# Router and transposes of a tile woven between the dense products of the next output projection unit

## The chip, the cores and the metric

One core of one Trainium2 chip runs the whole layer as one program. The metric is the device time of one execution in microseconds (us); the median of several runs is compared.

## The reference, cut to what matters

The kernel computes one encoder layer for two groups of tokens, 256 (prompt) and 512 (sample), that share all weights. The change lies in the second half of it:

```
def encoder_layer(x, ...):
    h = rms_norm(x, norm1_g)
    proj = h @ w_in                                     # 2048 -> 4896
    mla_out = mla_mixer(...)                            # 8 heads of 128
    gdn_out = gdn_mixer(...)                            # 8 heads of 128
    x = x + concatenate([mla_out, gdn_out]) @ w_o       # 2048 x 2048, the output projection
    x = x + ec_moe(rms_norm(x, norm2_g), w_router, w_gate, w_up, w_down)

def ec_moe(x, w_router, w_gate, w_up, w_down):
    C = 2 * T // 16                                     # 32 prompt, 64 sample tokens an expert
    aff = softmax(xt @ w_router)                        # T x 16
    gates, idx = top_k(aff.T, C)                        # each expert chooses its C tokens
    xe = xt[idx]
    h = silu(xe @ w_gate) * (xe @ w_up)                 # 16 experts, 2048 -> 1024
    ye = (h @ w_down) * gates
    out = zeros_like(xt).at[idx].add(ye)
```

All numbers are float32. The 16 experts' weights are 403 MB, read once.

## The kernel before

The 768 tokens are six tiles of 128. After the two mixers, `output_and_route` multiplies by w_o, adds the residual, normalises, computes the router's logits and lets each expert choose its tokens; `moe` then runs the experts one after another, their weights streamed in units of 2 MB through a ring of six buffers.

The output projection is cut into units (j, t): tile t of tokens by slice j of 512 columns of w_o, 16 matmuls with 128 rows of contraction each. Two records stand in the trace for one such matmul. The list `UNITS` has 24 of them, numbered u = 0 to 23: slice 0 of five tiles (four of which have only their last two contractions left), slices 1 to 3 of the same five tiles, and last the four slices of the sixth tile (ORDER[-1], tile 1), in the order 2, 3, 0, 1. `FIRST` is 15, the number of the first unit of slice 3: unit 15 + o finishes tile o of the order. Two buffers hold slices of w_o; slices 0 and 1 are therefore loaded a second time for units 22 and 23.

Each engine has its own program, written out by hand as a loop over the units; counting semaphores order them. Around a finished tile o this is the chain:

- TensorE: `accumulate(u)` (L1992), into PSUM bank u % 3.
- VectorE: `add(u)` (L2082) adds the residual. ScalarE: `square(u)` (L2193) sums squares, `rms(o)` (L2199, L2201) makes the scale.
- VectorE: `norm(o)` (L2094) writes the normed tile to `xn`, two buffers, both for the router and for the rows that go out.
- TensorE: `transposes(o)` (L2003), 16 transposes of 128 x 128 into PSUM banks 3 to 6, four to a bank; `store(o)` copies them to `xnT`, banks 3 and 5 on VectorE (L2103), 4 and 6 on ScalarE (L2208).
- TensorE: `router(o)` (L2014), 16 matmuls with 16 columns each, two records each, into bank 7. VectorE and ScalarE make the softmax (L2108 to L2120, L2214), `affinity(o)` (L2021) transposes it back.
- After five tiles, VectorE runs `top` (L2132 to L2135) for the sample tokens, eight rounds of maximum, index and replace. It stands ahead of the additions of units 22 and 23.
- The sixth tile is routed slice by slice by `last_transposes` (L2028) and `last_router` (L2042), then `top` runs for the prompt tokens.

The loop of TensorE before the change is, for each u: `accumulate(u)`; with o = u - 16 then `affinity(o - 2)`, `router(o - 1)`, `transposes(o)`, `last_transposes(o - 5)`, each where its index is in range. VectorE's order for each u is add, gain, softmax(o - 1), store(o), norm(o + 1), store_affinity(o - 2), top; ScalarE's is square, exponent(o - 1), store(o), rms(o + 1), store_last.

SyncE's program issues the DMAs in order: the residual, the slices of w_o, then for each tile `rows_out(o)` (L1945, L1946; waits for the norm of tile o, sends the normed and the plain rows, 1 MB each), and after `rows_out` of the fifth tile the second loads of slices 0 and 1, `load_w` (L1939), which wait until 21 and 22 units are done. Behind them come the first three units of expert 0, when unit 22 and unit 23 are done (L1972). The next units are requested by the following block, at L2338.

Of the kernel before, what the change touches and what calls it, by code (L numbers as in the profile page):

```python
# [20 lines left out]
P = 128  # L21
# [3 lines left out]
NT = T // P  # L25
TILES_P = SP_ // P
KD = D // P
# [3 lines left out]
H = 8  # L31
# [60 lines left out]
class Kernel:  # L92
# [18 lines left out]
    def sb(self, name, shape, dt=F32, ctx=None):  # L111
        return (ctx or self.ctx).enter_context(self.nc.sbuf_tensor(name, shape, dt))

    def sem(self, name, ctx=None):
        return (ctx or self.ctx).enter_context(self.nc.semaphore(name))
# [1738 lines left out]
def output_and_route(k):  # L1854

    nc, a, ps = k.nc, k.a, k.psum
# [20 lines left out]
    FIRST = (GR - 1) * (NT - 1)  # L1877
    done_at = lambda o: FIRST + o if o < NT - 1 else NU - 1
    with ExitStack() as c:
# [4 lines left out]
        xn = sb("xn", [P, 2, D])  # L1884
# [25 lines left out]
        s_acc = sem("output_projected")  # L1910
# [7 lines left out]
        s_tp = sem("xn_transposed")  # L1918
        s_td = sem("xnT_stored_vector")
        s_ta = sem("xnT_stored_scalar")  # L1920
        s_lg = sem("logits")
# [13 lines left out]
        with nc.Block() as block:  # L1935
# [43 lines left out]
            @block.tensor  # L1979
            def _(pe):  # L1980
                def accumulate(u):
                    j, t = UNITS[u]
                    if u == 0:
                        pe.wait_ge(k.s_mix, 32)
                    if u % (NT - 1) == 0 or u > GR * (NT - 1):
                        loads = 1 if j < 2 else 2
                        pe.wait_ge(s_w[j % 2], 16 * (loads if u <= GR * (NT - 1) or j >= 2 else 3))
                    if u >= 3:
                        pe.wait_ge(s_x2, u - 2)
                    q0 = PART_HEADS if j == 0 and t in PARTS else 0  # L1990
                    for q in range(q0, 2 * H):
                        last = nc.tensor.matmul(ps[:, u % 3, :], mixT[:, q, t * P:(t + 1) * P], wo[:, j % 2, q, :],  # L1992
                                                start=(q == q0), stop=(q == 2 * H - 1))
                    last.then_inc(s_acc, 1)

                def transposes(o):
                    pe.wait_ge(s_xn, o + 1)
                    for b in range(4):
                        if o:
                            pe.wait_ge((s_td, s_ta)[b % 2], 2 * o - 1 + b // 2)  # L2000
                        for j in range(4):
                            m = 4 * b + j
                            last = nc.tensor.transpose(ps[:, 3 + b, j * P:(j + 1) * P], xn[:, o % 2, m * P:(m + 1) * P], k.ident)  # L2003
                        last.then_inc(s_tp, 1)

                def router(o):
                    if o == 0:
                        pe.wait_ge(s_r, 48)
                    else:
                        pe.wait_ge(s_le, o)  # L2010
                    for q in range(KD):
                        if q % 4 == 0:
                            pe.wait_ge((s_td, s_ta)[(q // 4) % 2], 2 * o + 1 + q // 8)
                        last = nc.tensor.matmul(ps[:, 7, 0:NE], xnT[:, q, :], wr[:, q, :], start=(q == 0), stop=(q == KD - 1))  # L2014
                    last.then_inc(s_lg, 1)

                def affinity(o):
                    pe.wait_ge(s_af, o + 1)
                    if o:
                        pe.wait_ge(s_atc, o)  # L2020
                    nc.tensor.transpose(ps[0:NE, 7, P:2 * P], aff[:, ORDER[o], :], k.ident).then_inc(s_at, 1)  # L2021

                def last_transposes(p):
                    j = SLICES[p]
                    pe.wait_ge(s_xg, p + 1)
                    pe.wait_ge((s_td, s_ta)[j % 2], 2 * (NT - 1) - 1 + j // 2)
                    for m in range(4):
                        last = nc.tensor.transpose(ps[:, 3 + j, m * P:(m + 1) * P],  # L2028
                                                   xg[:, 512 * j + m * P:512 * j + (m + 1) * P], k.ident)
                    last.then_inc(s_tp, 1)  # L2030

                def last_router(p):
                    if p == 0:
                        pe.wait_ge(s_le, NT - 1)
                        pe.wait_ge(s_atc, NT - 1)
                    if p < 3:
                        pe.wait_ge(s_ta, 2 * (NT - 1) + p + 1)
                    else:
                        pe.wait_ge(s_td, 2 * (NT - 1) + 1)
                    for m in range(4):  # L2040
                        q = 4 * SLICES[p] + m
                        last = nc.tensor.matmul(ps[:, 7, 0:NE], xgT[:, q, :], wrp[:, q, :], start=(p == 0 and m == 0),  # L2042
                                                stop=(p == 3 and m == 3))
                    if p == 3:
                        last.then_inc(s_lg, 1)

                for u in range(NU):
                    accumulate(u)
                    o = u - FIRST - 1
                    if 2 <= o <= NT:  # L2050
                        affinity(o - 2)
                    if 1 <= o <= NT - 1:
                        router(o - 1)
                    if 0 <= o < NT - 1:
                        transposes(o)
                    if NT - 1 <= o <= NT:
                        last_transposes(o - NT + 1)
                pe.wait_ge(s_sel, 1)
                nc.tensor.transpose(ps[0:CS, 0, 0:NE], idxf[:, 0:CS], k.ident[0:NE, 0:NE]).then_inc(s_selt, 1)
                last_transposes(2)  # L2060
                last_router(0)
                last_router(1)
                last_transposes(3)
                last_router(2)
                last_router(3)
                affinity(NT - 1)
                pe.wait_ge(s_sel, 3)
                nc.tensor.transpose(ps[0:CP, 7, 256 + NE:256 + 2 * NE], idxf[:, CS:CT], k.ident[0:NE, 0:NE]).then_inc(s_selt, 1)
# [513 lines left out]
```

## Time and profile before

| | |
|---|---|
| median of 3 runs | 3069.76 us (3069.10 to 3069.83) |
| the profiled execution | 3071.65 us, span 3069.8 us |
| granted TensorE clock, mean | 0.976 of full speed |
| TensorE busy | 2891.6 us, 94% of the span |
| output projection and routing | 1625.4 to 1966.6 us |
| experts | 1966.6 to 3069.8 us |

The stretch that the change touches begins at 1813.14 (the first transposes) and ends at 1947.18. Times in rows are microseconds from the start of the span. The granted clock is 1.00 at 2.4 GHz and 0.50 at 1.2 GHz; PE is TensorE, PEld its weight loads, DVE VectorE, ACT ScalarE, SPq SyncE's queue of DMAs. In the rows the program's names of buffers stand: xT or xnT for transposed tiles, wbuf for the buffers that hold w_o and the expert weights, square for the identity matrix.

### The profile page before, as it was taken

The numbers are of one execution on the slowest core, as the hardware profiler recorded it, in microseconds if no ns is written. First come the engines' busy times: TensorE is split into PE (matmuls) and PEld (weight loads), VectorE is DVE, ScalarE is ACT, GpSimd is POOL, SyncE is SP. The second block draws the span as 40 slices with busy tenths as digits, with TensorE's granted clock in tenths as the row PEclk, the third lists the DMA queues.
The fourth block names the chain that finished last, engine by engine and source line by source line (L and its number), as shares of the span: only waits on it lengthen the run. The fifth ranks groups of instructions, "written<-read, shape, count | busy, mean of one in ns | idle before, by whom it ended". The sixth has DMA issues, their size and how long they took to land. (4 is left out here: it accounts for less than half of the span.)

```text
span 3069.8 us, 45507 instructions
## 1 busy us (share of the span) xinstructions
PE 2891.6 (94%) x19449; PEld 1451.7 (47%) x19449; DVE 890.9 (29%) x1613; ACT 512.7 (17%) x1333; POOL 409.8 (13%) x400
## 2 busy tenths in 40 slices
PE   8999999999999999998899999799999999999997
PEld 4544455555676666665564456333332232322232
DVE  1000344421764664675761022300000000000000
ACT  4110355412213213214111001100000000000000
POOL 0000111104114214215210000000110000011001
PEclk9999999999999999998999999899999999999998
DMA  5120200030211211103205113799999999999996
GB/s 184 55 73 21 68 28 28 11 118 28 56 53 38 56 42 49 56 15 118 72 22 212 55 55 155 289 404 397 386 390 381 395 395 394 393 394 387 391 396 250
DMA packets 140611, 561.01 MB, mean 183 GB/s; under 512 B 15216, under 2 KB 47816, under 8 KB 87240
## 3 DMA queue, kind: packets, MB, share of 16 engines
q1 hardware_dynamic: 131527, 534.08, 45.1%
q0 software_dynamic: 8960, 25.17, 3.9%
q8 instruction: 92, 1.51, 0.2%
q14 instruction: 32, 0.25, 0.0%
HBM read 524.25 MB, written 34.96 MB: 182 GB/s over the span
## 5 line engine op out<-in xcount | busy, mean ns | idle before, releaser
L2398 PE MATMUL psum<-wbuf,xeT 128*32 128x512 f32 x3120 | 356.8, 610 | 35.2 <-DMA wbuf<-in_w_up 32.3
L1222 PE MATMUL psum<-xT,wbuf 128*128 128x512 f32 x720 | 337.6, 606 | 0.3 <-PEq L612 0.3
L2398 PE MATMUL psum<-xT,xeT 128*32 128x512 f32 x3024 | 330.1, 592 | 0.0
L1992 PE MATMUL psum<-wbuf,xT 128*128 128x512 f32 x656 | 288.4, 601 | 1.0 <-PEq L1147 1.0
L460 PE MATMUL psum<-wbuf,xT 128*128 128x512 f32 (+1 forms) x704 | 281.1, 559 | 0.9 <-DVE xT L380 0.9
L2398 PEld LDWEIGHTS psum<-wbuf,xeT 128*32 128x32 f32 x3120 | 101.6, 113 | 283.6 <-issue 229.7
L2398 PEld LDWEIGHTS psum<-xT,xeT 128*32 128x32 f32 x3024 | 98.1, 110 | 226.4 <-issue 222.5
L1992 PEld LDWEIGHTS psum<-wbuf,xT 128*128 128x128 f32 x656 | 126.8, 195 | 157.6 <-issue 157.6
L460 PEld LDWEIGHTS psum<-wbuf,xT 128*128 128x128 f32 x704 | 133.4, 191 | 139.1 <-issue 120.0
L2481 DVE COPY hT<-psum 128x384 f32<-128x384 f32 x16 | 8.9, 557 | 646.9 <-PE psum L2381 646.9
L1222 PEld LDWEIGHTS psum<-xT,wbuf 128*128 128x128 f32 x720 | 132.1, 193 | 125.5 <-issue 120.5
L2418 PE MATMUL psum<-xT,hT 128*32 128x512 f32 x1584 | 173.2, 593 | 0.7 <-ACT hT L2453 0.7
L2453 ACT COPY hT<-psum 128x384 f32<-128x384 f32 x16 | 7.7, 479 | 971.8 <-PE psum L2381 971.8
L2418 PE MATMUL psum<-wbuf,hT 128*32 128x512 f32 x1488 | 164.3, 597 | 2.0 <-DVE hT L2481 2.0
L1225 PE MATMUL psum<-xT,wbuf 128*128 128x256 f32 x736 | 164.9, 379 | 0.0
L1225 PEld LDWEIGHTS psum<-xT,wbuf 128*128 128x128 f32 x736 | 138.7, 190 | 25.5 <-issue 8.1
L2542 POOL DMA_INDIRECT out_y_sample<-ye,scatter_rows x32 | 50.7, 1583 | 732.8 <-DVE ye L2495 727.9
L1290 PE MATMUL psum<-inv,mix_g 64*64 64x64 f32 (+1 forms) x2112 | 103.7, 230 | 38.1 <-DVE inv L1679 38.1
L1290 PEld LDWEIGHTS psum<-inv,mix_g 64*64 64x64 f32 (+1 forms) x2112 | 88.9, 141 | 93.8 <-DVE inv L1679 76.7
L1693 DVE TENSOR_TENSOR inv<-inv,psum 64x256 f32<-64x256 f32 (+1 forms) x264 | 116.9, 443 | 55.9 <-PE psum L1290 52.1
L1684 DVE TENSOR_TENSOR wbuf<-psum,blocks 128x512 f32<-128x512 f32 x144 | 96.6, 689 | 91.1 <-PE psum L1290 88.1
L2495 DVE TENSOR_SCALAR ye<-psum,gate 128x512 f32<-128x512 f32 x48 | 33.1, 745 | 305.1 <-PE psum L2418 305.1
(299 smaller groups left out, 3060.0 us busy)
## 6 DMA issues: line engine op xcount, KB each, us to landing
xT<-in_w_down SPq DMA_DIRECT2D x66, 1024.0 KB, 25.4
wbuf<-in_w_gate SPq DMA_DIRECT2D x65, 1024.0 KB, 20.1
wbuf<-in_w_up SPq DMA_DIRECT2D x65, 1024.0 KB, 23.5
xT<-in_w_gate SPq DMA_DIRECT2D x63, 1024.0 KB, 18.6
xT<-in_w_up SPq DMA_DIRECT2D x63, 1024.0 KB, 21.0
wbuf<-in_w_down SPq DMA_DIRECT2D x62, 1024.0 KB, 25.3
wbuf<-in_w_in SPq DMA_DIRECT2D x14, 2048.0 KB, 9.2
wbuf<-in_w_o SPq DMA_DIRECT2D x6, 4096.0 KB, 14.9
```

The costliest lines, as they stand in the source:

```text
L460: last = nc.tensor.matmul(ps[:, u % 3, 0:n], xT[:, d, t * P:(t + 1) * P], wb[g % 2][:, d, 0:n], start=(d == 0), stop=(d == KD - 1))
L1222: last = nc.tensor.matmul(ps[:, b, 0:SS_], wg[:, m % 2, d, h * P:(h + 1) * P], k.xT[:, d, SP_:T], start=(d == 0), stop=(d == KD - 1))
L1225: last = nc.tensor.matmul(ps[:, b + 1, 0:SP_], wg[:, m % 2, d, h * P:(h + 1) * P], k.xT[:, d, 0:SP_], start=(d == 0), stop=(d == KD - 1))
L1290: last = nc.tensor.matmul(ps[lo:hi, x, n * P + lo:n * P + hi], left[lo:hi, x, n, lo:hi], right[lo:hi, x, n, lo:hi], start=True, stop=True)
L1684: nc.vector.tensor_tensor(p1[:, x].rearrange("p (d h) c -> p d h c", d=2), ps[:, x, :].rearrange("p (d h c) -> p d h c", d=2, h=2), bcast( ...
L1693: last = nc.vector.tensor_tensor(o, o, bank[lo:hi, :, lo:hi], ALU.subtract)
L1992: last = nc.tensor.matmul(ps[:, u % 3, :], mixT[:, q, t * P:(t + 1) * P], wo[:, j % 2, q, :], start=(q == q0), stop=(q == 2 * H - 1))
L2398: last = nc.tensor.matmul(ps[32 * j:32 * j + 32, g, :].rearrange("p (x n) -> p x n", x=2), xeT[:, q, 32 * g:32 * g + 32], m[:, :, kk, 256 ...
L2418: last = nc.tensor.matmul(ps[32 * j:32 * j + 32, 3 + g, :], hT[:, f, 32 * g:32 * g + 32], m[:, kk, 512 * j:512 * j + 512], start=(f == 0), ...
L2481: nc.vector.tensor_copy(hidden(1), turned(1)).then_inc(s_hd, 1)
L2495: nc.vector.tensor_scalar(ye[:, g, :], ps[:, 3 + g, :], gate[:, g:g + 1], None, ALU.mult).then_inc(s_ye, 1)
L2542: nc.gpsimd.indirect_dma_start(y_s if 32 * g < CS else y_p, bass.IndirectOffsetOnAxis(ap=sq[:, g:g + 1], axis=0), ye[:, g, :], None, compu ...
```

## The change

`router` and `transposes` now take a second argument b, the group of four, and are called from inside `accumulate(u)` behind its dense matmuls number 1, 3, 5, 7 (router) and 9, 11, 13, 15 (transposes). In the loop they stood behind unit u; they are now inside unit u + 1, whose own index there is o = u - 17. The waits of the router that stood ahead of each fourth matmul stand ahead of each group. The signal that a unit is done is given with its last dense matmul, ahead of the last group of transposes. The programs of the other engines are unchanged.

```diff
--- before.py
+++ after.py
@@ -1988,31 +1988,36 @@
                     if u >= 3:
                         pe.wait_ge(s_x2, u - 2)
                     q0 = PART_HEADS if j == 0 and t in PARTS else 0
+                    o = u - FIRST - 2
                     for q in range(q0, 2 * H):
                         last = nc.tensor.matmul(ps[:, u % 3, :], mixT[:, q, t * P:(t + 1) * P], wo[:, j % 2, q, :],
                                                 start=(q == q0), stop=(q == 2 * H - 1))
-                    last.then_inc(s_acc, 1)
-
-                def transposes(o):
+                        if q == 2 * H - 1:
+                            last.then_inc(s_acc, 1)
+                        if q < 8 and q % 2 and 1 <= o <= NT - 1:
+                            router(o - 1, q // 2)
+                        if q >= 8 and q % 2 and 0 <= o < NT - 1:
+                            transposes(o, q // 2 - 4)
+
+                def transposes(o, b):
                     pe.wait_ge(s_xn, o + 1)
-                    for b in range(4):
-                        if o:
-                            pe.wait_ge((s_td, s_ta)[b % 2], 2 * o - 1 + b // 2)
-                        for j in range(4):
-                            m = 4 * b + j
-                            last = nc.tensor.transpose(ps[:, 3 + b, j * P:(j + 1) * P], xn[:, o % 2, m * P:(m + 1) * P], k.ident)
-                        last.then_inc(s_tp, 1)
-
-                def router(o):
-                    if o == 0:
+                    if o:
+                        pe.wait_ge((s_td, s_ta)[b % 2], 2 * o - 1 + b // 2)
+                    for j in range(4):
+                        m = 4 * b + j
+                        last = nc.tensor.transpose(ps[:, 3 + b, j * P:(j + 1) * P], xn[:, o % 2, m * P:(m + 1) * P], k.ident)
+                    last.then_inc(s_tp, 1)
+
+                def router(o, b):
+                    if o == 0 and b == 0:
                         pe.wait_ge(s_r, 48)
-                    else:
+                    elif b == 0:
                         pe.wait_ge(s_le, o)
-                    for q in range(KD):
-                        if q % 4 == 0:
-                            pe.wait_ge((s_td, s_ta)[(q // 4) % 2], 2 * o + 1 + q // 8)
+                    pe.wait_ge((s_td, s_ta)[b % 2], 2 * o + 1 + b // 2)
+                    for q in range(4 * b, 4 * b + 4):
                         last = nc.tensor.matmul(ps[:, 7, 0:NE], xnT[:, q, :], wr[:, q, :], start=(q == 0), stop=(q == KD - 1))
-                    last.then_inc(s_lg, 1)
+                    if b == 3:
+                        last.then_inc(s_lg, 1)
 
                 def affinity(o):
                     pe.wait_ge(s_af, o + 1)
@@ -2049,10 +2054,6 @@
                     o = u - FIRST - 1
                     if 2 <= o <= NT:
                         affinity(o - 2)
-                    if 1 <= o <= NT - 1:
-                        router(o - 1)
-                    if 0 <= o < NT - 1:
-                        transposes(o)
                     if NT - 1 <= o <= NT:
                         last_transposes(o - NT + 1)
                 pe.wait_ge(s_sel, 1)
```

## Rows read from the trace of the kernel before

**Rows 1.** The page: engines, and the costliest group of part 5.

```profile
PE 2891.6 (94%) x19449; PEld 1451.7 (47%) x19449; DVE 890.9 (29%) x1613; ACT 512.7 (17%) x1333; POOL 409.8 (13%) x400
...
L2398 PE MATMUL psum<-wbuf,xeT 128*32 128x512 f32 x3120 | 356.8, 610 | 35.2 <-DMA wbuf<-in_w_up 32.3
```

**Rows 2.** Timeline of TensorE: start, duration, engine, line, operation.

```profile
1813.14 1.91 PE L2003 MATMUL psum<-square,xn 128*128 128x128 f32 x16
1814.89 13.90 PE L1992 MATMUL psum<-wbuf,xT 128*128 128x512 f32 x32
1828.62 4.32 PE L2014 MATMUL psum<-wr,xnT 128*128 128x16 f32 x32
1832.79 3.65 PE L2003 MATMUL psum<-square,xn 128*128 128x128 f32 x16
1836.23 14.88 PE L1992 MATMUL psum<-wbuf,xT 128*128 128x512 f32 x32
...
1851.07 3.64 PE L2014 MATMUL psum<-wr,xnT 128*128 128x16 f32 x32
1854.56 2.98 PE L2003 MATMUL psum<-square,xn 128*128 128x128 f32 x16
...
1947.18 0.20 PE L2059 MATMUL psum<-square,top_idx 16*64 16x16 f32 x1
```

**Rows 3.** Windows: stretch, us, engines' busy us; last clock, DMA share, GB/s.

```profile
1813.10:1947.20 134.10, 134.10 (x479) 77.92 (x477) 49.88 (x94) 15.18 (x44) 0.00 (x0) 0.92 0.40 157
1896.10:1899.50 3.40, 3.40 (x18) 3.40 (x18) 1.91 (x6) 0.95 (x3) 0.00 (x0) 0.52 1.05 404
1899.50:1913.30 13.80, 13.80 (x34) 6.07 (x33) 0.28 (x2) 0.59 (x1) 0.00 (x0) 0.99 0.44 162
```

**Rows 4.** Timeline of TensorE and windows, the stage before the projection.

```profile
1596.81 1.88 PE L1363 MATMUL psum<-wbuf,xT 128*128 128x512 f32 x4
1598.53 1.05 PE L1326 MATMUL psum<-wbuf,tf 128*128 128x128 f32 x8
1599.42 1.88 PE L1363 MATMUL psum<-wbuf,xT 128*128 128x512 f32 x4
...
1594.00:1612.00 18.00, 18.00 (x101) 12.73 (x101) 5.85 (x18) 1.82 (x4) 2.34 (x4) 1.00 0.28 88
1174.00:1181.00 7.00, 4.24 (x20) 2.70 (x20) 6.75 (x7) 5.84 (x11) 0.00 (x0) 1.00 0.04 16
```

**Rows 5.** Timeline of TensorE: matmuls behind a wait (in brackets).

```profile
322.11 4.54 PE L521 MATMUL psum<-wq,qlT 128*128 128x384 f32 x8 [2.68 <-DVE qraw L784]
...
2381.58 5.36 PE L2398 MATMUL psum<-wbuf,xeT 128*32 128x512 f32 x48 [2.59 <-DMA wbuf<-in_w_up]
...
2860.42 7.92 PE L2398 MATMUL psum<-wbuf,xeT 128*32 128x512 f32 x48 [3.66 <-DMA wbuf<-in_w_up]
```

**Rows 6.** Timeline of VectorE, behind the transposes of the second tile.

```profile
1837.53 3.77 DVE L2094 SCALAR_TENSOR_TENSOR xn<-x,rs_d,g 128x2048 f32<-128x2048 f32 x1 [1.15 <-ACT rs_d L2201]
```

**Rows 7.** SyncE's queue and DMA windows; then issue to landing of the load.

```profile
1883.51 0.32 SPq L1945 DMA_DIRECT2D xn_prompt<-xn  x1
...
1892.73 0.38 SPq L1939 DMA_DIRECT2D wbuf<-in_w_o  x1
...
1884.20:1889.40 5.20, 5.20 (x13) 2.28 (x12) 0.00 (x0) 0.00 (x0) 0.00 (x0) 1.00 0.97 403
1894.40:1905.40 11.00, 11.00 (x47) 7.85 (x48) 2.20 (x7) 1.54 (x4) 0.00 (x0) 0.84 1.01 375
...
wbuf<-in_w_o SPq DMA_DIRECT2D x1, 4096.0 KB, 14.5
```

**Rows 8.** Timeline of VectorE around the search for the sample tokens.

```profile
1917.32 0.18 DVE L2108 TENSOR_REDUCE lmax<-psum 128x1 f32<-128x16 f32 x1 [2.38 <-PE psum L2014]
...
1937.42 0.27 DVE L2125 COPY affT<-psum 16x128 f32<-16x128 f32 x1
```

**Rows 9.** Windows: the first part of the experts.

```profile
1970.00:2218.00 248.00, 245.10 (x2258) 80.45 (x2260) 17.51 (x29) 8.99 (x17) 21.76 (x27) 0.98 1.02 394
```

## The prediction

> **What bounds the kernel now.** I read the page first: TensorE is busy 94% of the span [rows 1]. Then the timeline of TensorE over the output projection: from the first transposes at 1813.14 to the first instruction behind the last unit at 1947.18 it never stands still [rows 2]. So here TensorE itself sets the end, and only shorter work or a faster clock helps. One period is dense group, affinity transpose, router, transposes. Look at the same piece of work in two periods: 16 transposes take 1.75 us (1813.14 to 1814.89) and 3.44 us (1832.79 to 1836.23). The granted clock says why: 0.52 in a stretch of transposes, 0.99 in the dense group behind it, 0.92 over all 134.1 us [rows 3]. Each router batch, 32 records of 16 columns behind one another, is where the clock falls from 2.4 to 1.2 GHz; the low stretch reaches into the transposes and the first dense matmuls.
>
> Behind the projection comes a tail of vector and DMA work, then the experts. There the DMA engines are full, share 1.02 from 1970 on [rows 9], and the costliest group of the page waits 32.3 us for in_w_up [rows 1]. An expert phase limited by bytes ends as much earlier as it starts earlier, because its fourth to sixth units are only requested when the projection block is over. So whatever the projection gains arrives at the end one for one, and a faster clock among the experts gives nothing.
>
> **The change, part by part.** No instruction is added or removed; per unit the same 16 dense matmuls, 32 router records, 16 transposes.
>
> (a) Price of the pieces at full clock. Eight dense matmuls: half of 13.73 us (1814.89 to 1828.62), 6.87. A router batch 3.49 (1851.07 to 1854.56), four transposes 1.75/4 = 0.44, an affinity transpose a quarter of that, 0.11 [rows 2]. What does chopping cost? Before, nearly the same weave stands at 1596.81: two dense matmuls (4 records) until 1598.53, 1.72 us, then 8 records of 128 columns until 1599.42, 0.89 us [rows 4]. The unchopped router would have 3.49/4 = 0.87 for such a group, so chopping costs 0.02 a group. A router half is then 4 x (1.72 + 0.89) = 10.44, a transpose half 4 x (1.72 + 0.44) = 8.64.
>
> (b) The sum from 1813.14 on, all at full clock: unit 17 (transposes only) 6.87 + 8.64 = 15.5; units 18 to 21, 4 x 19.08 = 76.3; unit 22 (router only) 10.44 + 6.87 = 17.3; unit 23, two halves of 6.87, 13.7; five affinity transposes 0.6; two groups of last_transposes 0.9. Together 124.3 against 134.0 now: a gain of 9.7. Without the cost of chopping (20 router groups by 0.02) it is 10.1; the clock's 0.08 of 134.1 would be 10.7. I take 9.8, bounds 9.0 and 10.7.
>
> (c) Does the clock stay up? In the new weave TensorE never has more than 0.89 us of thin work before 1.72 us dense. In the weave of [rows 4] the clock stood at 1.00, but its thin groups have 128 columns, not 16. A nearer bound from below: 1174 to 1181, where TensorE was busy 4.24 of 7.00 us with a hole of 2.76, also 1.00 [rows 4]. I take full clock; a low clock is a rival below.
>
> (d) Later transposes. They now end with their unit, so what hangs on them moves. Scalar stores groups 1 and 3 and only then computes rms(o+1); the norm of the next tile on Vector waits for it. In the old period the next dense group starts at 1836.23 [rows 2] and the norm runs 1837.53 + 3.77, to 1841.30: 5.1 us after the transposes [rows 6]. The old kernel did this under a dense group, and for transposes(o+1), 11 us into the next unit, it still is in time. The add of the finished unit waits behind it on Vector, 5 us late; its PSUM bank is needed two units later, so that costs nothing.
>
> (e) SyncE's queue is where it hurts. rows_out(4) needs norm 4, and load_w(0), the weight slice of unit 22, is queued behind it. Today norm 4 is long done: rows_out(4) goes out at 1883.51, and load_w(0) at 1892.73 just as unit 20 ends [rows 7]. Call E the end of the transposes in unit 20. After the change norm 4 is ready at E + 5.1, rows_out moves 2 MB until 5.9 us after its issue (data 1884.2 to 1889.4 for an issue at 1883.51), then the 4 MB slice: it landed 14.5 us after issue, of which the first 1.7 passed before data ran at full rate (1894.4), so 12.8; the data alone ran 11.0 [rows 7]. Landing is at E + 5.1 + 5.9 + 11.0 to 12.8 = E + 22.0 to 23.8. TensorE wants it at E + 0.11 + 19.08 + 0.11 + 0.44 = E + 19.7. That is a new wait of 2.3 to 4.1 us; I take 3.3, nearer the end with the landing in it. Its bounds are 0 (if the rows overlap the load) and 5 (if the rows and the slice disturb each other). Queued behind it on TensorE is all of unit 22 with the last router, hence everything to the end. load_w(1), 11.0 us of data more, has until E + 40 and is hidden.
>
> (f) Such a hole can drop the clock. Of 12 waits of 2.5 to 4.0 us in this trace that found TensorE at full speed, 8 were followed by a fall (the first at 322.11, the last at 2860.42); one that was not is 2381.58, where 48 records took 5.36 us against 7.92 [rows 5]. A fall costs 1.7 (a stretch of 3.4 us at half speed, as the transposes of [rows 3]) to 2.6 us (7.92 against 5.36). I take 1.7, since it is of this stage.
> On this a rule of the Trainium skill can be weighed. The row: in 1896.10 to 1899.50 only transposes ran, at 0.52, and the dense stretch behind shows 0.99, so the clock was back within 0.3 us of it [rows 3]; transposes had kept TensorE awake. The Trainium skill, "TensorE: Matmul & The Clock Gate", Part 4 (PE-mode transpose), says that transpose mode doesn't count as TensorE activity. By that rule the two groups of transposes just ahead of the hole are quiet too and the fall is nearly sure (3065.0); by the row it is a matter of phase.
>
> (g) The search. softmax(4) and the eight rounds of top hang on the last router, which moves to 6.87 us of dense work before the end of unit 22. The chain from the router's end (lmax at 1917.32, 0.2 after it) to the last store at 1937.42 + 0.27 is 20.6 us [rows 8]. Behind the router TensorE still has 6.87 + 0.11 + 0.44 + 13.7 = 21.1 us. It fits, with 0.5 us to spare; nothing of the old cover is left. If it didn't, each microsecond late would go to the end.
>
> Sum: -9.8 + 3.3 + 1.7 = -4.8. The profiled execution took 3071.65 (span 3069.8), 1.9 above the median 3069.76; the difference is applied to the median: 3065.0.
>
> **The rivals.** A: the above, 3065.0, its own range 3063.4 to 3066.5. 0.43.
> B: the hole at unit 22, no fall: 3069.76 - 9.8 + 3.3 = 3063.3. For it 4 of 12 waits. 0.25.
> C: the slice lands in time, for instance because its descriptors run beside the writes: 3060.0. Against it: DMA share in both transfers is already about 1, so two cannot overlap. 0.16.
> D, slower: 16 columns per record are too thin, and the clock falls in the router halves. Two stretches of 3.4 us at half speed in each of five units lose 5 x 3.4 = 17 us against full clock: 3069.76 - 9.8 + 17 + 3.3 = 3080.3. It decides from where more than 2 x (9.8 - 3.3) = 13 us of the stretch run at half speed. Against it [rows 4]; for it that no row shows thin work of just this width woven in. 0.05.
> E, the change doesn't do what it says: the clock falls as often as today, and the longer units hide most of the hole: about 3070. 0.07.
> F: the search is late by 1 to 3 us on top of A: 3067. 0.04.
>
> **How the numbers follow.** The time is that of A, 3065.0. The range 3059.8 to 3068.0 takes A, B, C and F and leaves out D, E. A change of 0.2% (6.1 us, 3063.6) is about what a measurement of this kernel tells from none. Faster: most of C (0.15), two thirds of B (0.16), the edge of A (0.05), 0.36. Slower: D, 0.05. The same: 0.59.
>
> **What would show it.** Granted clock of 1.00 in units 17 to 21, and 16 woven transposes at 1.75 us together (a, b, c); the norm 5.1 us behind the transposes (d); load_w(0) issued about 6 us after unit 20's end, and a wait of about 3 us of TensorE for in_w_o ahead of unit 22 (e); half clock just behind it (f); the add of unit 23 not later than 0.1 us after its matmuls (g); the chain from there to the first expert matmul 25.3 us as now. Wrong I am if the hole is absent, or the clock falls while the weave runs.

## The result and the profile after

The changed kernel takes 3077.99 us (median of 9 runs, 3070.35 to 3081.39) against 3069.10 of the kernel before (9 runs, 3066.28 to 3071.36): ratio 1.0026, 95% interval 1.0016 to 1.0037, so 5 to 11 us slower. A second set of runs (e8 below) gave the ratio 1.0027 (1.0016 to 1.0038). The prediction was 3065.0, range 3059.8 to 3068.0; it had the wrong sign. Its 5% for "slower", rival D at 3080.3, was on another mechanism: that 3078 lies near D's figure is coincidence.

The page first, its first section for the engines:

```profile
span 3079.6 us, 45519 instructions
## 1 busy us (share of the span) xinstructions
PE 2895.2 (94%) x19449; PEld 1448.6 (47%) x19449; DVE 890.3 (29%) x1613; ACT 512.3 (17%) x1333; POOL 409.5 (13%) x400
```

The counts of TensorE are those of [rows 1]; no work was added. Now TensorE's waits from 1800 to 1990 of the changed kernel (engine, waiting line, releaser: total us, times, longest):

```profile
PE psum L2026 <- DVE affT L2126: 10.1, 2, 5.0
PE psum L2426 <- DVE replicated L2500: 7.1, 1, 7.1
PE psum L2069 <- DVE top_idx L2179: 6.0, 1, 6.0
PE psum L2026 <- DVE aff L2121: 2.0, 1, 2.0
```

The last three lines belong to the tail and stand there before, too. The first is new. Nothing of the kind was in [rows 2], where TensorE ran without a gap. The timeline of TensorE shows where it stands, and that the weave around it runs as planned:

```profile
1851.85 0.27 PE L2026 MATMUL psum<-square,aff 128*16 128x128 f32 x1
1851.96 1.88 PE L1993 MATMUL psum<-wbuf,xT 128*128 128x512 f32 x4
1853.68 0.96 PE L2018 MATMUL psum<-wr,xnT 128*128 128x16 f32 x8
1854.49 1.96 PE L1993 MATMUL psum<-wbuf,xT 128*128 128x512 f32 x4
...
1870.58 0.60 PE L2008 MATMUL psum<-square,xn 128*128 128x128 f32 x4
1876.21 0.27 PE L2026 MATMUL psum<-square,aff 128*16 128x128 f32 x1 [5.03 <-DVE affT L2126]
1876.34 3.52 PE L1993 MATMUL psum<-wbuf,xT 128*128 128x512 f32 x4
1879.66 1.13 PE L2018 MATMUL psum<-wr,xnT 128*128 128x16 f32 x8
...
1902.36 0.37 PE L2026 MATMUL psum<-square,aff 128*16 128x128 f32 x1 [5.03 <-DVE affT L2126]
1902.53 3.71 PE L1993 MATMUL psum<-wbuf,xT 128*128 128x512 f32 x4
1906.04 1.73 PE L2018 MATMUL psum<-wr,xnT 128*128 128x16 f32 x8
1907.60 3.50 PE L1993 MATMUL psum<-wbuf,xT 128*128 128x512 f32 x4
```

The affinity transposes of the second and the third tile wait 5.03 us each. The first, at 1851.85, doesn't. The same four dense records take 1.88 us ahead of a hole and 3.52 or 3.71 behind it. The windows say that this is the clock (columns as in [rows 3]):

```profile
1825.80:1870.80 45.00, 45.00 (x188) 26.19 (x187) 14.37 (x21) 5.89 (x17) 0.00 (x0) 1.00 0.23 94
1870.90:1876.20 5.30, 0.28 (x3) 0.06 (x2) 3.93 (x3) 0.98 (x3) 0.00 (x0) 1.00 0.00 0
1876.20:1880.00 3.80, 3.79 (x8) 1.72 (x8) 0.46 (x1) 0.72 (x2) 0.00 (x0) 0.55 0.87 356
...
1902.30:1911.00 8.70, 8.64 (x19) 4.72 (x19) 1.20 (x2) 0.72 (x2) 0.00 (x0) 0.52 0.94 329
1911.00:1957.90 46.90, 46.90 (x171) 25.26 (x169) 22.93 (x58) 4.19 (x12) 0.00 (x0) 1.00 0.67 253
```

In the weave 1.00, where [rows 3] had 0.92 over the whole; behind the holes 0.55 for 3.8 us and 0.52 for 8.7 us.

What is VectorE doing in the first hole? Its timeline, with one row of ScalarE's behind:

```profile
1869.07 0.69 DVE L2104 COPY xnT<-psum 128x512 f32<-128x512 f32 x1 [3.55 <-PE psum L2008]
1869.67 0.15 DVE L2088 TENSOR_REDUCE ss_d<-ssp 128x1 f32<-128x4 f32 x1
1872.27 3.69 DVE L2095 SCALAR_TENSOR_TENSOR xn<-x,rs_d,g 128x2048 f32<-128x2048 f32 x1 [2.45 <-ACT rs_d L2202]
1875.81 0.26 DVE L2126 COPY affT<-psum 16x128 f32<-16x128 f32 x1
...
1871.22 0.58 ACT L2209 COPY xnT<-psum 128x512 f32<-128x512 f32 x1 [3.67 <-PE psum L2008]
```

The transposes end at about 1871.0. Only then can ScalarE store the fourth group (1871.22) and compute the scale, VectorE run the norm of the next tile (1872.27 to 1875.96), and behind it in VectorE's program the small copy of the previous tile's affinities (L2126). TensorE's next affinity transpose overwrites the place from which that copy reads, so it waits for it. Before the change the same norm and the same copy were over 9.2 us ahead of that need. VectorE, then TensorE's transpose of the second tile's affinities:

```profile
1858.63 3.77 DVE L2094 SCALAR_TENSOR_TENSOR xn<-x,rs_d,g 128x2048 f32<-128x2048 f32 x1 [1.15 <-ACT rs_d L2201]
1862.25 0.27 DVE L2125 COPY affT<-psum 16x128 f32<-16x128 f32 x1
...
1871.75 0.27 PE L2021 MATMUL psum<-square,aff 128*16 128x128 f32 x1
```

**Where the microseconds are.** Cut each profiled span at the start of unit 0, at the end of unit 23 and at the first expert matmul:

| kernel | to unit 0 | units 0 to 23 | tail | experts | span |
|---|---|---|---|---|---|
| before | 1625.4 | 321.8 | 25.3 | 1097.3 | 3069.8 |
| changed | 1629.5 | 328.5 | 25.3 | 1096.4 | 3079.6 |
| changed, second profile (e8) | 1627.1 | 328.4 | 25.5 | 1096.3 | 3077.3 |

The change is in the second column: +6.6 us (328.46 less 321.81 before rounding), the same in two executions. The first and the last column move by some microseconds between executions of any of these kernels (1621 to 1629 and 1091 to 1098 over ten profiles), which is why the profile of the changed kernel lies 9.8 us above that of before, and why stretches are compared below beside medians. To rounding, the 6.6 us come apart as -9.8 for the weave at full clock (measured in e2, below), +10.1 for the two holes, and a rest of 6.4. Of this rest 5.9 is the low clock behind the holes, where the work from 1876.21 to 1880.63 and from 1902.36 to 1910.94 took 5.9 us more than the same groups at 1.00.

### The profile page after: what moved, and what is told of

Same layout as the page of the kernel before. It is cut to its first block and busy times, and to the rows that moved or that the text cites. A ratio compares the mean times of both kernels' runs of the same rounds, so it can differ in the third digit from the quotient of the medians.

```text
span 3079.6 us, 45519 instructions
## 1 busy us (share of the span) xinstructions
PE 2895.2 (94%) x19449; PEld 1448.6 (47%) x19449; DVE 890.3 (29%) x1613; ACT 512.3 (17%) x1333; POOL 409.5 (13%) x400
## 5 line engine op out<-in xcount | busy, mean ns | idle before, releaser
L1993 PE MATMUL psum<-wbuf,xT 128*128 128x512 f32 x656 | 297.6, 607 | 1.0 <-PEq L1147 1.0
L1225 PEld LDWEIGHTS psum<-xT,wbuf 128*128 128x128 f32 x736 | 138.7, 190 | 25.5 <-issue 8.1
```

The lines of the kernel that those rows point to most:

```text
L1225: last = nc.tensor.matmul(ps[:, b + 1, 0:SP_], wg[:, m % 2, d, h * P:(h + 1) * P], k.xT[:, d, 0:SP_], start=(d == 0), stop=(d == KD - 1))
```

## The experiments

All but e7 start from the changed kernel; e4, e5 and e6 have the edit of e3 as well. e1 to e4 and e5 to e8 each had their own runs of the kernel before (medians 3069.92 and 3069.98); ratios are against those.

| run | median us (runs) | ratio to before, 95% | units 0 to 23, us |
|---|---|---|---|
| e1 affinities stored before the norm | 3068.04 (11) | 0.9995 (0.9986 to 1.0004) | 321.7 |
| e2 the same, slice of w_o loaded first | 3062.01 (7) | 0.9969 (0.9958 to 0.9981) | 312.0 |
| e3 norm early | 3058.98 (5) | 0.9961 (0.9947 to 0.9974) | 312.1 |
| e4 norm early, router alone woven | 3056.98 (5) | 0.9960 (0.9946 to 0.9974) | 311.8 |
| e5 norm early, transposes alone woven | 3072.77 (12) | 1.0013 (1.0004 to 1.0022) | 323.7 |
| e6 norm early, router by eight | 3061.93 (11) | 0.9971 (0.9961 to 0.9980) | 312.0 |
| e7 kernel before, norm early | 3070.79 (11) | 1.0004 (0.9995 to 1.0013) | 321.8 |
| e8 changed kernel again | 3076.77 (7) | 1.0027 (1.0016 to 1.0038) | 328.4 |

**e1, the affinities stored ahead of the norm.** Is the new wait the cause? VectorE's order alone is changed:

```diff
                         softmax(o - 1)
+                    if 2 <= o <= NT:
+                        store_affinity(o - 2)
                     if 0 <= o < NT - 1:
                         store(o)
                     if 0 <= o + 1 < NT - 1:
                         norm(o + 1)
-                    if 2 <= o <= NT:
-                        store_affinity(o - 2)
```

> The changed kernel, but on VectorE store_affinity stands right behind the softmax and no longer behind the norm. Theory 1 (TensorE stood twice for 5.03 us at the affinity transpose, because the store that frees its place was queued behind a norm that now ends 5 us after the unit, and each hole was followed by a low clock): both holes go, and the clock is 1.00 there; TensorE reaches the last unit early enough to meet the late slice of w_o, a wait of 2.5 to 4 us for in_w_o ahead of unit 22. Time 9.8 - 3.3 us under the kernel before, 3062.6, or 3064.3 with a fall behind the wait. Theory 2 (chopping the weave itself costs the 9 us): time stays at 3076 to 3078.

Measured 3068.04 against 3069.92, which is above the 3062.6 or 3064.3 expected. Both waits of 5 us are gone. In their place stands the one that the prediction had named. TensorE's timeline and windows, then SyncE's queue:

```profile
1908.85 0.60 PE L2033 MATMUL psum<-square,xn 128*128 128x128 f32 x4
1914.24 3.78 PE L1993 MATMUL psum<-wbuf,xT 128*128 128x512 f32 x4 [4.78 <-DMA wbuf<-in_w_o]
1917.81 1.73 PE L2018 MATMUL psum<-wr,xnT 128*128 128x16 f32 x8
1919.38 3.76 PE L1993 MATMUL psum<-wbuf,xT 128*128 128x512 f32 x4
...
1914.20:1924.00 9.80, 9.76 (x24) 5.64 (x24) 0.00 (x0) 0.00 (x0) 0.00 (x0) 0.52 0.96 354
...
1894.62 0.32 SPq L1945 DMA_DIRECT2D xn_prompt<-xn  x1
1894.98 0.43 SPq L1946 DMA_DIRECT2D out_y_prompt<-x  x1
1895.46 13.42 SPq L1939 DMA_DIRECT2D wbuf<-in_w_o  x2
...
wbuf<-in_w_o SPq DMA_DIRECT2D x1, 4096.0 KB, 18.7
```

Unit 20 ended at 1889.57. The rows went out 5.05 us later (predicted 5.1), the slice landed 18.7 us after its own issue, and TensorE stood for 4.78 us (predicted 3.3, within the bound of 5), then ran 9.8 us at 0.52. Theory 2 (3076 to 3078) falls; theory 1 stands, with the hole and above all the clock behind it dearer than expected: 321.7 - 312.0 = 9.7 us in all, 4.8 of hole and 4.9 of clock.

**e2, the load ahead of the rows as well.** In SyncE's program, `rows_out` of the fifth tile moves behind the first load:

```diff
-                for o in range(NT - 1):
+                for o in range(NT - 2):
                     rows_out(o)
                 for j in (0, 1):
                     sp.wait_ge(s_acc, GR * (NT - 1) + 1 + j)
                     load_w(j)
+                    if j == 0:
+                        rows_out(NT - 2)
```

> As e1, and in SyncE's queue the load of slice 0 of w_o stands ahead of the rows of the fifth tile. Theory 1: no hole is left at unit 22 either, the stretch from the first transposes' unit to the end of unit 23 runs at full clock, 9.8 us under the kernel before: 3059.3. If the wait for w_o of e1 isn't there because the slice lands in time, e1 and e2 agree within 1 us. Theory 2: 3076 to 3078.

Measured 3062.01, ratio 0.9969. The median is 2.7 us above the expected 3059.3; the ratio is worth 9.5 us, with an interval of 6 to 13, and the 9.8 forecast lies inside. The stretch shows it more sharply: 312.0 against 321.8, 9.8 us. No wait is left in it, and the clock is 1.00:

```profile
1813.00:1936.90 123.90, 123.90 (x478) 69.12 (x476) 49.59 (x94) 15.16 (x44) 0.00 (x0) 1.00 0.44 170
...
1935.24 0.69 DVE L2148 TENSOR_TENSOR xn<-x,g 128x512 f32<-128x512 f32 x1
1935.85 0.27 DVE L2128 COPY affT<-psum 16x128 f32<-16x128 f32 x1
1936.99 0.69 DVE L2085 TENSOR_TENSOR x<-psum,x 128x512 f32<-128x512 f32 x1 [0.87 <-PE psum L1995]
```

The lower three rows are VectorE at the end of unit 23: the search and what follows it are over 0.87 us before the last addition can start. Step (g) of the prediction gave 0.5.

**e3, one edit instead of two.** VectorE's norm and ScalarE's rms stand first, directly behind add and square:

```diff
+                    if 0 <= o + 1 < NT - 1:
+                        norm(o + 1)
                     if 1 <= o <= NT - 1:
                         softmax(o - 1)
                     if 0 <= o < NT - 1:
                         store(o)
-                    if 0 <= o + 1 < NT - 1:
-                        norm(o + 1)
...
+                    if 0 <= o + 1 < NT - 1:
+                        rms(o + 1)
                     if 1 <= o <= NT - 1:
                         exponent(o - 1)
                     if 0 <= o < NT - 1:
                         store(o)
-                    if 0 <= o + 1 < NT - 1:
-                        rms(o + 1)
```

> The changed kernel, but VectorE's norm and ScalarE's rms of the next tile stand right behind the addition and the squares, ahead of softmax and stores. It takes the late norm away, which theory 1 names as the one cause of the holes and of the late rows in SyncE's queue: no hole at the affinity transposes, none at unit 22, time as e2, 3059.3 (within 1.5 us). Theory 2: 3076 to 3078.

Measured 3058.98, ratio 0.9961, expected 3059.3. The stretch is 312.1 us without a wait. So the late norm is the common cause of both kinds of hole.

**e4 and e5, one half of the weave each,** both with the norm early. e4 takes the two lines that call `transposes` out of `accumulate` and puts a loop over its four groups behind the unit; e5 does so with the router:

```diff
-                        if q < 8 and q % 2 and 1 <= o <= NT - 1:
-                            router(o - 1, q // 2)
...
+                    if 1 <= o <= NT - 1:
+                        for b in range(4):
+                            router(o - 1, b)
```

> As e3, but only the router is woven; the sixteen transposes of a tile stand in one block behind the unit, as before. The clock theory (only the router's thin batch lets the clock fall; transposes keep it up): granted clock 1.00 throughout, time as e3, 3059.3. Against it (a block of 16 transposes is quiet too and costs clock by itself): 1 to 1.7 us lost in each of five units, 3064 to 3068.

> As e3 (norm early), but the router of a tile stands in one block of 32 thin records behind the unit, as in the kernel before, and only the transposes are woven. Clock theory (the gain of the weave is the clock that the router's batch lets fall): a fall with each of the five router blocks, 1.7 us each or up to 8.5 us in all, time 3059.0 + 8.5 = 3067 (3064 to 3068). Rival (the gain comes from the weaving of either part, or from the early norm): within 1.5 us of e3, 3059.

e4 measured 3056.98, stretch 311.8 us; e5 3072.77, stretch 323.7. The windows of e4 over all its woven units, and TensorE with its windows in e5:

```profile
1812.90:1937.20 124.30, 124.30 (x478) 69.88 (x476) 49.83 (x94) 14.64 (x44) 0.00 (x0) 1.00 0.44 169
```

```profile
1847.42 3.64 PE L2016 MATMUL psum<-wr,xnT 128*128 128x16 f32 x32
1850.91 5.38 PE L1993 MATMUL psum<-wbuf,xT 128*128 128x512 f32 x8
...
1847.40:1850.90 3.50, 3.50 (x34) 3.50 (x33) 1.92 (x3) 1.71 (x5) 0.00 (x0) 1.00 0.00 0
1850.90:1857.50 6.60, 6.60 (x14) 2.86 (x14) 2.91 (x5) 0.36 (x2) 0.00 (x0) 0.74 0.53 218
```

A block of sixteen transposes costs no clock; with a block of 32 thin router records the clock falls each time. Eight dense records take 5.38 us behind it, against 3.60 at full clock in e6. The gain of the change is thus the weaving of the router alone. The price of its absence, 323.7 - 312.1 = 11.6 us against e3, is more than the 8.5 that I expected, and the time lies above the 3064 to 3068 expected. The reason can be read from the timeline: three of the five falls cost 1.7 to 1.8 us each, the first and the last 3.4. In the kernel before, the first fall cost 3.4 and the other four 1.7 each. That is why e5, with its transposes woven, takes 1.9 us longer in this stretch than the kernel before.

**e6, the router in groups of eight** behind dense matmuls 3 and 7:

```diff
-                        if q < 8 and q % 2 and 1 <= o <= NT - 1:
-                            router(o - 1, q // 2)
+                        if q in (3, 7) and 1 <= o <= NT - 1:
+                            router(o - 1, q // 2 - 1)
+                            router(o - 1, q // 2)
```

> As e3, but the router is woven in groups of eight products (16 records, 1.75 us) behind dense matmuls 3 and 7 instead of four behind 1, 3, 5, 7. If the clock bears a thin stretch of 1.75 us between 3.4 us of dense work: 1.00 throughout and the time of e3, 3059, at most 0.2 us less for fewer switches. If the limit lies below 1.75 us: falls in the router halves, up to 1.7 us for each of five units, up to 3067.

Stretch 312.0 us as in e2 and e3, clock 1.00 over its woven units. The median, 3061.93, is 2.9 us above the expected 3059; by the stretch, whose spread is smaller, nothing was lost. A thin run of 1.7 us is borne between 3.5 us of dense work (timeline of TensorE, e6):

```profile
1855.11 1.85 PE L2019 MATMUL psum<-wr,xnT 128*128 128x16 f32 x16
1856.82 3.68 PE L1993 MATMUL psum<-wbuf,xT 128*128 128x512 f32 x8
1860.33 1.85 PE L2019 MATMUL psum<-wr,xnT 128*128 128x16 f32 x16
```

**e7, the kernel before with the early norm** (the edit of e3), and **e8, the changed kernel again.**

> The kernel before with nothing changed but VectorE's norm and ScalarE's rms of the next tile directly behind addition and squares. Theory 1: the norm is hidden under the next unit there either way, so no change, 3069.9 within 1.5 us, and the gain of e3 over the kernel before is that of the weave. Rival (the early norm is worth something by itself): 3062 or less.

> The changed kernel itself once more beside the others, for a profile of another execution. Theory 1: again two waits of TensorE of 5.0 us at the affinity transposes of the second and third tile, none at unit 22, and a low clock behind them that differs with the execution; time 3078 (3075 to 3081). If the first profile was a chance: waits of another number or length.

e7: 3070.79, ratio 1.0004, stretch 321.8; the early norm is worth nothing without the weave. e8: 3076.77, two waits of 5.03 us at the same two places, stretch 328.4. The low clock behind them was expected to differ with the execution; it didn't (four dense records took 3.53 and 3.71 us, against 3.52 and 3.71).

## Why the prediction was wrong

- **What bounds the stretch: right.** TensorE sets it, and gains and losses there reach the end: the tail is 25.3 to 25.5 us in all ten profiles.
- **(a), (b) the price of the pieces: right.** A gain of 9.8 us was taken; e2 shows 321.8 - 312.0 = 9.8.
- **(c) the clock in the weave: right.** 1.00 in all woven stretches of e2, e3, e4 and e6, and of the changed kernel outside its holes. Rival D, the one on the slow side, isn't what happened.
- **(d) later transposes: here it failed.** "The add of the finished unit waits behind it on Vector, 5 us late; its PSUM bank is needed two units later, so that costs nothing." The time of the norm was right (5.1 predicted, 1871.0 to 1875.96 measured), and the late add by itself is indeed free: in e1 it is as late, and the two holes are gone. But the add isn't all that is queued behind the norm: `store_affinity(o - 2)` stands between them, in my own list of VectorE's order, and `affinity(o - 1)` on TensorE waits for it at once. I followed one instruction behind the late one and not each. Two units have both a norm ahead of the store and a following affinity that waits; the first tile's has no such wait, and after the fifth tile there is no norm. That is 10.1 us, and with the clock 16.5.
- **(e) the slice of w_o: right as a mechanism, hidden in the changed kernel.** There the slice, issued at 1902.97, landed 19.8 us later, at 1922.8, and the holes of (d) had put TensorE's need for it off to 1926.22. Without them it appears, at 4.78 us instead of 3.3. The term that was short is from issue to landing: behind 2 MB of rows the slice took 18.7 us, where mine comes to 16.1 to 17.9 (5.9 + 11.0 to 12.8 from the issue of the rows, less 0.84 to its own).
- **(f) the clock behind a hole: right that it falls, too cheap.** I took 1.7 us, with 2.6 as the dear end. It was 4.9 us behind the hole of e1, and 6.4 for the two of the changed kernel. The low stretches were 9.8 us at 0.52 in e1, 3.8 and 8.7 in the changed kernel. The rows I priced it by had only transposes and dense matmuls in the low stretch, where here thin router groups stand in it; whether these draw it out isn't shown.
- On the rule of the Trainium skill, "TensorE: Matmul & The Clock Gate", Part 4 (PE-mode transpose): its statement that transposes don't count as activity doesn't fit what was seen, though no run isolates it. [rows 3] have the clock come back at the end of a stretch of nothing but transposes, and the falls behind the second to fourth router batch cost 1.7 to 1.8 us each whether transposes stand in them (the kernel before) or only dense matmuls (e5). That blocks of 16 transposes leave the clock at 1.00 in e4 agrees, but proves little by itself: they last 1.75 us, and e6 bears 1.7 us of thin work too.
- **(g) the search: right,** 0.87 us to spare.

With (d) priced, and the wait of (e) hidden by it, the sum would have been -9.8 + 10.1 and 1.7 to 5.2 for the clock (one fall at 1.7 to two at 2.6), 3071.8 to 3075.3: still under the 3078 measured, but with the right sign.

What stays open: why the clock's low stretch behind the first hole of the changed kernel is 3.8 us and behind the second 8.7, alike in both profiles. No run was made to part hole length from what follows it.

## What to carry to other kernels

When a step is moved later, write down for each engine everything that its program queues behind the instruction that waits for it, down to the smallest copy, and ask for each who needs it next; a copy of 0.26 us behind a norm cost more here than all that the weave gained. Put the work that can start early (norm) ahead of the work that waits for another engine (stores) in an in-order queue: one reordering (e3) turned 6.6 us lost in this stretch into 9.7 won. Thin matmuls (16 columns) are worth breaking up between dense ones when they run back to back for 3.5 us; blocks of 16 transposes (1.75 us) were not.

## What the runs showed of the hardware

A batch of 3.5 us of 16-column products drops TensorE from 2.4 to 1.2 GHz, five times of five (e5); runs of 1.7 us between dense work never do (e6), nor do blocks of 16 full transposes (e4). Such a fall cost 1.7 to 1.8 or 3.4 us. Each of the three waits of about 5 us (two in the changed kernel, one in e1), and each of the two in e8, was followed by 3.8 to 9.8 us at the low level; with that the one of e1 cost 9.7 us, the two of the changed kernel 16.5. Behind two writes of 1 MB from the same queue, a load of 4 MB took 18.7 us to land (e1; 19.8 in the changed kernel, 18.5 in e8), against 14.5 alone [rows 7] and 14.4 ahead of the writes (e2).
